# A decoder trunk in split precision: three quarters of the second layer's input turned outside TensorE, and a weight's splits spread out

## The chip, the cores and the metric

The kernel runs on one core of a Trainium2 chip. The metric is device microseconds for one execution of the whole program (two layers); lower is better. Three runs of the kernel before gave 887.66, 887.83 and 887.92 us, median 887.83.

## The reference, cut to what matters

Two layers, each of which maps `x` (256 tokens x 2048 columns) to `LayerNorm(alpha * x + y)`. `y` comes from one wide projection of `x` whose columns go to four groups of heads (retention, latent attention, an mLSTM cell, cross-attention to a fixed memory of 256 tokens), a gate, and one output projection:

```
h = x @ w_in                                   # split into the groups' inputs
cq = rmsnorm(h[a_cq]) ; q = cq @ w_uq          # latent attention: 384 "compressed query" columns, w_uq is 384 x 768
memo = softmax(c_q @ k_mem.T / sqrt(128)) @ v_mem,   k_mem, v_mem = split(mem @ w_mem_kv)
y = (concat(ret, mla, mls, memo) * silu(z)) @ w_out
x = layernorm(2 ** 0.5 * x + y, ln_g, ln_b)    # input of the next layer
```

All values are float32. The second layer needs the first one's normalised output transposed (columns on the partitions), because a matmul contracts over the partitions.

## The kernel before, in words

**Split products.** TensorE multiplies in a rounded 32-bit format. To keep precision each operand is split in a high part (ScalarE rounds it by a copy) and a low part (VectorE subtracts the high part from the operand), and each product is three matmuls: high x high, low x high, high x low.

**Chunks and tiles.** The weights of a layer are streamed as a row of chunks: `memv` (tiles 0 to 15), `memk` (16 to 31), the feature-major halves `lx0 lx1 cq0 cq1` (32 to 63), `akv` (64 to 79, 256 columns wide), `aq` (80 to 95, 328 wide), `lv` (96 to 111), `lo` (112 to 127) and so on, 304 tiles a layer. A tile is 128 rows of a chunk, in most chunks 512 columns wide. SP loads two tiles at a time (a pair, number m holds tiles 2m and 2m + 1) into a buffer of four pairs, in order, together with all other transfers. ScalarE writes a tile's high part (L1095), VectorE its low part (L1446), into rings of five tiles; TensorE uses them in order (L1357, L1358 for the high part, L1361 for the low one; L1372 and L1378 in the feature-major chunks). A slot of the ring is written again when TensorE is through with it. So ScalarE and VectorE run ahead of TensorE by less than five tiles, and every engine works strictly in the order of its own program.

**An order written out by hand.** All other work is a set of steps that are put behind numbered tiles: `PE_AT`, `ACT_AT` and `DVE_AT` give for each engine the tile behind whose own work a step stands (`FIRST_` and `LATER_` hold for one layer alone). Steps at the same tile run in the order in which `_put` entered them. Steps that matter here, with their tiles:
- `wuq` k (k = 0, 1, 2): the copy L937 on ScalarE (behind tiles 45, 46, 47) and the subtraction L1566 on VectorE (behind 46, 47, 48) that split a third of the compressed queries' weight, 128 x 768 values. The product that needs all three (`mla_qr`) stands behind tile 132.
- `ml_fold` (L1179 on TensorE behind 72, copied out by ScalarE, L1004, behind 77).
- the memory heads h = 0 to 3: `mem_scores` on TensorE behind 71, 75, 81, 87; `mem_max` on VectorE (L1587, L1589) behind 76, 80, 86, 92; `mem_exp` on ScalarE (L954) behind 78, 82, 88, 94; `mem_norm` on VectorE (L1594, L1597) behind 80, 84, 90, 96; a turn of each head on VectorE (L1578) behind 81, 85, 93, 97. ScalarE's `mem_pT` copies behind 102, 103, 110 and 111 wait for a transfer. VectorE's `turn c` stands behind 109.

**The second layer's input.** The first layer's output `X` (two halves of 128 tokens, four column blocks of 512) is normalised by ScalarE in eight steps (`normalise`, L868) behind tiles 8 to 15 of the second layer, while TensorE works on the memory chunks, which don't need it. Columns 0 to 1023 are turned by TensorE: steps `xT` 0 and 1 behind tile 18, `xT` 2 and 3 behind tile 22, each four transposes of 128 x 128 (L1131) into one bank of `work`. Columns 1024 to 2047 go another way: VectorE turns each 32 x 32 square in place (`square_x` 2 and 3, L1517, two instructions each), SP writes the result to DRAM (behind pairs 10 and 11) and reads it back with the squares in their places (behind pairs 14 and 15, four reads of 32 partitions each, after both writes have landed). ScalarE then makes `xx`'s high part (`x_hi` j behind tiles 23, 24, 27, 28, 29, 30, 32, 33, L890: gain and bias of the norm in the same instruction) and VectorE the low part (`x_lo` j behind tiles 24 to 37, L1500, L1509), j running over blocks of 256 columns. The chunk `lx0` is the first that needs them.

Of the kernel before, what the change touches and what calls it, by code (L numbers as in the profile page):

```python
# [29 lines left out]
F32 = mybir.dt.float32  # L30
# [6 lines left out]
P = 128  # L37
DEPTH = 2
D_MODEL = 2048
SEQ = 256  # L40
# [93 lines left out]

for _j in range(4):
    _put(LATER_PE, 18 + _j // 2 * 4, "xT", _j)
# [18 lines left out]
for _j in range(8):  # L155
    _put(LATER_ACT, 8 + _j, "normalise", (4, 5, 6, 7, 0, 1, 2, 3)[_j])
    _put(LATER_ACT, (23, 24, 27, 28, 29, 30, 32, 33)[_j], "x_hi", _j)
    _put(FIRST_ACT, 15 + 2 * _j, "x_hi", _j)
    if _j:
        _put(FIRST_ACT, 2 * _j - 1, "m_hi", _j + 1)  # L160
# [26 lines left out]
DVE_AT = {}  # L187
_put(LATER_DVE, 11, "square_x", 2)
_put(LATER_DVE, 13, "square_x", 3)
for _j in range(8):  # L190
# [126 lines left out]
def build_trunk(nc, a, out):  # L317
    ctx = ExitStack()
    with ctx:
# [139 lines left out]

        x_squares, x_turned = ([B[i][:, 0:1024] for i in pair] for pair in ((4, 5), (2, 0)))  # L460

        def x_block(j, n):

            return x_turned[j // 2 - 2].rearrange("p (a i j r) -> p j i a r", a=4, i=NT, j=4)[:, j % 2 * 2 + n]

# [80 lines left out]
        scaled, copied = signal("scaled", 0), signal("copied", 0)  # L546
        x_squared, x_turn_out = signal("x_squared", 0), signal("x_turn_out", 0, step=16)
        stored = signal("stored", 0, step=16)
# [134 lines left out]
        def _(sp):  # L683
            for l in range(DEPTH):
                for m in range(PAIRS):
# [61 lines left out]
                    if m == 57:  # L747
# [3 lines left out]
                          .then_inc(mrow_in.sem, 16)  # L751
                    if l and m in (10, 11):
                        sp.wait_ge(x_squared.sem, m - 9)
                        sp.dma_start(a["x_turn"][m - 10], x_squares[m - 10]).then_inc(x_turn_out.sem, 16)
                    if l and m in (14, 15):
                        sp.wait_ge(x_turn_out.sem, 2 * 16)
                        for b in range(4):
                            sp.dma_start(x_turned[m - 14][b * 32:(b + 1) * 32, :].rearrange("c (a n) -> c a n", a=4),
                                         a["x_turn"][m - 14, :, b * 256:(b + 1) * 256].rearrange("(a c) n -> c a n", a=4))\
                              .then_inc(xT_in[m - 12].sem, 16)  # L760
# [79 lines left out]
        def _(act):  # L840
# [20 lines left out]
            for l in range(DEPTH):  # L861

                def normalise(b):
                    cb, i = divmod(b, 2)
                    blk = X[:, i, cb * 512:(cb + 1) * 512]
                    if b == 4:
# [10 lines left out]
                def x_hi_(j):  # L877
                    if l == 0:
                        act.wait_ge(xT_in[j // 2].sem, 16)
                        act.activation(xh[:, 2 * j:2 * j + 2, :], xT0[:, j, :].rearrange("p (k t) -> p k t", k=2),  # L880
                                       ACT.Copy).then_inc(x_hi.sem, 1)
                        return
                    if j < 4:
                        wait_job(act, l, ("xT", j))
                    else:
                        act.wait_ge(xT_in[j // 2].sem, 16 + 4 * 16)
                    act.wait_ge(cols_in.sem, cols_in.at(l, 0))
                    for k in (2 * j, 2 * j + 1):
                        o, f = xh[:, k, :], (bank(l, ("xT", j))[:, (k % 2) * 256:(k % 2 + 1) * 256] if j < 4 else x_block(j, k % 2))
                        m = act.activation(o if j < 4 else o.rearrange("p (i a r) -> p i a r", i=NT, a=4), f, ACT.Identity,  # L890
                                           scale=cols[:, C_LNG + k:C_LNG + k + 1], bias=cols[:, C_LNB + k:C_LNB + k + 1])
                    m.then_inc(x_hi.sem, 1)
# [223 lines left out]
        def _(pe):  # L1116
# [5 lines left out]
            for l in range(DEPTH):  # L1122
# [295 lines left out]
        def _(dve):  # L1418
# [49 lines left out]
            for l in range(DEPTH):  # L1468
# [23 lines left out]
                def x_lo_(j):  # L1492
                    dve.wait_ge(x_hi.sem, x_hi.at(l, j))
                    src, part = xT0[:, j, :].rearrange("p (k t) -> p k t", k=2), xh[:, 2 * j:2 * j + 2, :].bitcast(F32)
                    if l:
                        dve.wait_ge(cols_in.sem, cols_in.at(l, 0))
                        for k in (2 * j, 2 * j + 1):
                            o, f = tmp[:, (k % 2) * 256:(k % 2 + 1) * 256], \
                                (bank(l, ("xT", j))[:, (k % 2) * 256:(k % 2 + 1) * 256] if j < 4 else x_block(j, k % 2))
                            m = dve.tensor_scalar(o if j < 4 else o.rearrange("p (i a r) -> p i a r", i=NT, a=4), f,  # L1500
                                                  cols[:, C_LNG + k:C_LNG + k + 1], cols[:, C_LNB + k:C_LNB + k + 1],
                                                  ALU.mult, ALU.add)
                        if j < 4:
                            m.then_inc(free_bank(l, "xT", j), 1)
                            wait_read(dve, l, ("xT", j))
                        else:
                            link(m)
                        src = tmp[:, :].rearrange("p (k t) -> p k t", k=2)
                    dve.tensor_tensor(xl[:, 2 * j:2 * j + 2, :], src, part, ALU.subtract).then_inc(x_lo.sem, 1)  # L1509
                    if l:  # L1510
                        dve.wait_ge(x_lo.sem, x_lo.at(l, j))

                def square_x(cb):
                    dve.wait_ge(normed.sem, 2 * cb - 2)
                    to = x_squares[cb - 2].rearrange("p (b i j r) -> p i j b r", b=4, i=NT, j=4)
                    for i in range(NT):
# [3 lines left out]
                def gain(b):  # L1520
                    cb, i = divmod(b, 2)
                    blk = X[:, i, cb * 512:(cb + 1) * 512]
                    if b == 0:
                        dve.wait_ge(gb0_in.sem, 16)
                        wait_job(dve, l, ("xT", 3))
                    link(dve.tensor_tensor(blk, blk, gb0[:, 0, cb * 512:(cb + 1) * 512], ALU.mult))
# [585 lines left out]
```

## Time and profile before

| | |
|---|---|
| median of three runs | 887.83 us |
| the profiled execution: its time, its span | 888.09 us, 886.3 us |
| TensorE busy | 880.4 us, 99% of the span |
| VectorE busy | 665.6 us, 75% |
| ScalarE busy | 488.4 us, 55% |
| transfers | 200.33 MB, mean 226 GB/s |

The span runs from the first to the last instruction; the time of the execution holds 1.8 us outside it. Records of successive instructions on one engine overlap by some 0.1 us, on TensorE by more, as its matmuls are pipelined and their ends modelled: what an instruction takes from its engine is read from the distance of two starts. `[2.14 <-PE acc L1361]` behind a row says that the engine stood idle for 2.14 us before it and what ended this.

### The profile page before, as it was taken

How to read it: one execution, taken by the hardware profiler on the slowest of the kernel's cores; microseconds unless marked ns; L12 is line 12 of the kernel's file. 1: busy time of each engine (PE TensorE's matmuls, PEld its weight loads, DVE VectorE, ACT ScalarE, POOL GpSimd, SP SyncE). 2: the span in 40 equal slices, each digit the busy share in tenths (PEclk: the TensorE clock that was granted, in tenths of full speed). 3: DMA queues.
4: the chain of work that ended last, by engine and by line, in shares of the span. 5: the costliest groups of instructions: out<-in, count | busy, mean ns of one | idle time of the engine just before them, and what ended most of it. 6: DMA issues, size and time to landing. Idle time of an engine off the chain costs nothing.

```text
span 886.3 us, 13162 instructions
## 1 busy us (share of the span) xinstructions
PE 880.4 (99%) x4508; PEld 756.2 (85%) x4508; DVE 665.6 (75%) x1326; ACT 488.4 (55%) x914; POOL 18.0 (2%) x18
## 2 busy tenths in 40 slices
PE   9999999999999999999999999999999999999997
PEld 8888998888888888888888889888888888888896
DVE  6869697878695677766679787968777878786765
ACT  6655776545455346544477556755355453565641
POOL 0000000000000000000000000000000001000001
PEclk9999999999999999999999999999999999999999
DMA  9796487547769677566577866884485865867832
GB/s 358 294 324 205 135 263 257 185 141 222 225 222 312 216 245 256 199 198 194 194 237 232 297 252 176 267 261 167 144 266 163 278 228 161 289 218 258 320 89 95
DMA packets 72402, 200.33 MB, mean 226 GB/s; under 512 B 9608, under 2 KB 24208, under 8 KB 71696
## 3 DMA queue, kind: packets, MB, share of 16 engines
q1 hardware_dynamic: 71760, 198.44, 67.9%
q10 hardware_dynamic: 576, 1.05, 0.4%
q8 instruction: 36, 0.59, 0.3%
q14 instruction: 30, 0.25, 0.1%
HBM read 183.43 MB, written 16.00 MB: 225 GB/s over the span
## 4 chain that ended last, share of the span: by engine, by line
PE 98%; issue 1%; DMA 0%; ACT 0%; POOL 0%; DVE 0%; POOLq 0%; ACTq 0%; DVEq 0%
PE acc L1357 24%; PE acc L1358 24%; PE acc L1361 24%; PE acc L1372 10%; PE acc L1378 5%; PE work L1138 1%; PE work L1137 1%; PE work L1136 1%; PE work L1262 1%; DMA B<-in_mem_t 0%; PE work L1285 0%; PE work L1274 0%; PE work L1194 0%; PE work L1188 0%; PE acc L1398 0%
## 5 line engine op out<-in xcount | busy, mean ns | idle before, releaser
L1095 ACT ACTIVATE hi<-raw 128x512 fp32r<-128x512 f32 (+2 forms) x607 | 356.3, 604 | 300.3 <-PE acc L1361 242.5
L1446 DVE TENSOR_TENSOR lo<-raw,hi 128x512 fp32r<-128x512 f32 (+2 forms) x607 | 387.2, 655 | 176.7 <-ACT hi L1095 167.8
L1357 PE MATMUL acc<-hi,xx 128*128 128x512 f32 (+2 forms) x768 | 285.5, 374 | 0.0
L1358 PE MATMUL acc<-hi,xx 128*128 128x512 f32 (+2 forms) x768 | 283.6, 372 | 0.0
L1361 PE MATMUL acc<-lo,xx 128*128 128x512 f32 (+2 forms) x768 | 223.0, 372 | 0.0
L1357 PEld LDWEIGHTS acc<-hi,xx 128*128 128x128 f32 x768 | 144.6, 188 | 23.6
L1358 PEld LDWEIGHTS acc<-hi,xx 128*128 128x128 f32 x768 | 144.6, 188 | 23.6
L1361 PEld LDWEIGHTS acc<-lo,xx 128*128 128x128 f32 x768 | 140.4, 188 | 24.6
L1372 PE MATMUL acc<-xx,hi 128*128 128x512 f32 x384 | 96.0, 392 | 0.0
L1372 PEld LDWEIGHTS acc<-xx,hi 128*128 128x128 f32 x384 | 69.3, 189 | 12.6
L1378 PEld LDWEIGHTS acc<-xx,lo 128*128 128x128 f32 x384 | 52.4, 190 | 3.7
L1378 PE MATMUL acc<-xx,lo 128*128 128x256 f32 x384 | 53.5, 282 | 0.0
L1357 PE MATMUL acc<-hi,mm 128*128 128x512 f32 x126 | 49.2, 391 | 0.0
L1358 PE MATMUL acc<-hi,mm 128*128 128x512 f32 x126 | 49.0, 389 | 0.0
L1361 PE MATMUL acc<-lo,mm 128*128 128x512 f32 x126 | 38.8, 389 | 0.0
L1361 PEld LDWEIGHTS acc<-lo,mm 128*128 128x128 f32 x126 | 23.6, 188 | 5.0
L1357 PEld LDWEIGHTS acc<-hi,mm 128*128 128x128 f32 x126 | 23.7, 188 | 4.8
L1358 PEld LDWEIGHTS acc<-hi,mm 128*128 128x128 f32 x126 | 23.7, 188 | 4.8
L816 POOL TENSOR_TENSOR rstd<-stats,half 128x4 f32<-128x4 f32 (+1 forms) x6 | 9.6, 1594 | 349.0 <-DVE stats L1899 220.5
L997 ACT ACTIVATE B<-work 128x512 f32<-128x512 f32 x12 | 7.2, 596 | 14.7 <-PE work L1138 14.7
L1622 DVE SCALAR_TENSOR_TENSOR B<-B,cols 128x256 f32<-128x256 f32 x24 | 11.6, 482 | 0.6
L1358 PE MATMUL acc<-hi,B1r 128*128 128x512 f32 (+1 forms) x32 | 12.0, 377 | 0.0
(355 smaller groups left out, 960.1 us busy)
## 6 DMA issues: line engine op xcount, KB each, us to landing
raw<-in_w SPq DMA_DIRECT2D x263, 512.0 KB, 4.3
B<-turn SPq DMA_DIRECT2D x80, 128.0 KB, 4.6
raw<-in_w SPq DMA_DIRECT2D x26, 256.0 KB, 2.7
turn<-B SPq DMA_DIRECT2D x12, 512.0 KB, 5.8
raw<-in_w SPq DMA_DIRECT2D x16, 328.0 KB, 3.3
turn<-Y SPq DMA_DIRECT2D x8, 512.0 KB, 5.6
Y<-in_wuq SPq DMA_DIRECT2D x2, 1152.0 KB, 8.3
Y<-in_x_t SPq DMA_DIRECT2D x4, 512.0 KB, 8.7
```

Of the source, the lines that this page charges most:

```text
L816: return pool.tensor_tensor(dst, src, half[:, 0:n], ALU.pow)
L1095: act.activation(place(l, t, hi), raw[:, s, (t % 2) * w:(t % 2 + 1) * w], ACT.Copy)\
L1136: pe.matmul(o, ah, bh, start=start, stop=False)
L1137: pe.matmul(o, al, bh, start=False, stop=False)
L1138: return pe.matmul(o, ah, bl, start=False, stop=stop)
L1357: pe.matmul(o, ah[:, q], hi[:, s, 0:w], start=k == 0, stop=False, skip_group_check=name == "memv")
L1358: pe.matmul(o, al[:, q], hi[:, s, 0:w], start=False, stop=False, skip_group_check=name == "memv")
L1361: m = pe.matmul(acc[:, p, i, 0:w], ah[:, i * P:(i + 1) * P], lo[:, s, 0:w], start=False, stop=k == KT - 1, skip_group_check=name == "memv")
L1372: pe.matmul(acc[:, p, j, :], hi[:, (l * SLOTS + t + u) % RING, q], x, start=k + u == 0 and kk == 0, stop=False, skip_group_check=True)
L1378: m = pe.matmul(acc[:, p, j, 0:SEQ], lo[:, s, q], both_parts[:, 2 * k + kk, 0, :], start=False, stop=2 * k + kk == KT - 1, skip_group_chec ...
L1446: dve.tensor_tensor(place(l, t, lo), raw[:, s, (t % 2) * w:(t % 2 + 1) * w], place(l, t, hi).bitcast(F32), ALU.subtract).then_inc(lo_done. ...
L1622: m = dve.scalar_tensor_tensor(xcT[:, j, :], LX[:, j, tap:tap + SEQ], wcol, xcT[:, j, :], ALU.mult, ALU.add)
```

## The change

It does two things. The column block 512 to 1023 of the second layer's input takes the way of squares and DRAM as well, so that three blocks go that way and TensorE turns only columns 0 to 511 (`xT` 0 and 1). The normalisation begins with the blocks that go this way; the squares stand behind tiles 10, 12 and 14, the writes behind pairs 10, 11 and 12, the reads behind pairs 13, 14 and 15, each of which waits for its own block's write alone. `xT` waits for all eight normalisations.

And in both layers the three splits of the compressed queries' weight move: the copies to tiles 77, 108 and 118, the subtractions to tiles 79, 109 and 120. They are entered after the other steps at the same tile (`ml_fold` at 77 on ScalarE, `turn c` at 109 and `ml_gap` 3 at 120 on VectorE).

```diff
-for _j in range(4):
+for _j in range(2):
     _put(LATER_PE, 18 + _j // 2 * 4, "xT", _j)
...
-    _put(LATER_ACT, 8 + _j, "normalise", (4, 5, 6, 7, 0, 1, 2, 3)[_j])
+    _put(LATER_ACT, 8 + _j, "normalise", (2, 3, 4, 5, 6, 7, 0, 1)[_j])
...
-_put(LATER_DVE, 11, "square_x", 2)
-_put(LATER_DVE, 13, "square_x", 3)
+for _cb in range(1, 4):
+    _put(LATER_DVE, 8 + 2 * _cb, "square_x", _cb)
...
 for _k in range(3):
-    _put(ACT_AT, 45 + _k, "wuq", _k)
-    _put(DVE_AT, 46 + _k, "lo", "wuq", _k)
+    _put(ACT_AT, (77, 108, 118)[_k], "wuq", _k)
+    _put(DVE_AT, (79, 109, 120)[_k], "lo", "wuq", _k)
...
-        x_squares, x_turned = ([B[i][:, 0:1024] for i in pair] for pair in ((4, 5), (2, 0)))
+        x_squares, x_turned = ([B[i][:, 0:1024] for i in pair] for pair in ((4, 5, 6), (7, 2, 0)))
...
-                    if l and m in (10, 11):
+                    if l and m in (10, 11, 12):
                         sp.wait_ge(x_squared.sem, m - 9)
-                        sp.dma_start(a["x_turn"][m - 10], x_squares[m - 10]).then_inc(x_turn_out.sem, 16)
-                    if l and m in (14, 15):
-                        sp.wait_ge(x_turn_out.sem, 2 * 16)
+                        sp.dma_start(a["x_turn"][m - 10], x_squares[m - 10]).then_inc(x_turn_out[m - 10].sem, 16)
+                    if l and m in (13, 14, 15):
+                        sp.wait_ge(x_turn_out[m - 13].sem, 16)
                         for b in range(4):
...
-                    if j < 4:
+                    if j < 2:
                         wait_job(act, l, ("xT", j))
                     else:
                         act.wait_ge(xT_in[j // 2].sem, 16 + 4 * 16)
...
-                    pe.wait_ge(normed.sem, 2 * (j // 2) + 6)
+                    pe.wait_ge(normed.sem, 2 * (j // 2) + 8)
```

## Rows read from the trace of the kernel before

**Rows 1.** Busy time by engine, page part 1, cut to its one line.

```profile
PE 880.4 (99%) x4508; PEld 756.2 (85%) x4508; DVE 665.6 (75%) x1326; ACT 488.4 (55%) x914; POOL 18.0 (2%) x18
```

**Rows 2.** TensorE's waits: us in total, times, longest.

```profile
PE work L1120 <- DVE half L1420: 1.1, 1, 1.1
...
```

**Rows 3.** TensorE's timeline, layer 2, tiles 17 to 19: start us, us, instructions.

```profile
464.33 0.39 PE L1357 MATMUL acc<-hi,mm 128*128 128x512 f32 x1
...
465.69 1.04 PE L1131 MATMUL work<-ident,X 128*128 128x128 f32 x8
...
467.95 0.40 PE L1357 MATMUL acc<-hi,mm 128*128 128x512 f32 x1
```

**Rows 4.** Instructions of line 1131: duration ns least/median/most, first and last start.

```profile
L1131 PE MATMUL work<-ident,X x16: 270/272/273, 465.7 to 472.8; 128*128 128x128 f32 x16
```

**Rows 5.** VectorE's timeline, layer 2, squares behind tile 13.

```profile
453.56 1.30 DVE L1517 STREAM_TRANSPOSE B<-X 128x512 f32<-128x512 f32 x2
...
455.67 0.69 DVE L1446 TENSOR_TENSOR lo<-raw,hi 128x512 fp32r<-128x512 f32 x1 [0.24 <-ACT hi L1095]
```

**Rows 6.** SP's timeline, layer 2: the first turned block is read back.

```profile
465.55 2.80 SPq L758 DMA_DIRECT2D B<-x_turn  x4
```

**Rows 7.** DMA issues: count, KB each, median us from issue to landing.

```profile
B<-x_turn SPq DMA_DIRECT2D x8, 128.0 KB, 4.9
```

**Rows 8.** ScalarE's timeline, layer 2, behind tile 27.

```profile
472.79 1.00 ACT L890 ACTIVATE xx<-work,cols 128x256 fp32r<-128x256 f32 x2
```

**Rows 9.** ScalarE's timeline, layer 1: splits at tiles 46 and 47; tiles 77 to 79.

```profile
66.23 0.83 ACT L937 ACTIVATE Xr<-Y 128x768 fp32r<-128x768 f32 x1
66.97 0.62 ACT L1095 ACTIVATE hi<-raw 128x512 fp32r<-128x512 f32 x1
...
102.81 0.60 ACT L1004 ACTIVATE B<-work 128x512 f32<-128x512 f32 x1 [0.48 <-PE work L1179]
103.58 0.42 ACT L1095 ACTIVATE hi<-raw 128x256 fp32r<-128x256 f32 x1 [0.17 <-PE acc L1361]
...
106.23 1.51 ACT L1095 ACTIVATE hi<-raw 128x256 fp32r<-128x256 f32 x4
```

**Rows 10.** VectorE's timeline, layer 1: tiles 46, 47, 79 to 81, 91.

```profile
67.23 0.95 DVE L1566 TENSOR_TENSOR Yr<-Y,Xr 128x768 fp32r<-128x768 f32 x1
68.09 0.69 DVE L1446 TENSOR_TENSOR lo<-raw,hi 128x512 fp32r<-128x512 f32 x1
...
106.68 0.86 DVE L1446 TENSOR_TENSOR lo<-raw,hi 128x256 fp32r<-128x256 f32 x2 [2.22 <-ACT hi L1095]
107.46 0.16 DVE L1594 RECIPROCAL rinv<-rsum 128x2 f32<-128x2 f32 x1
...
108.98 0.50 DVE L1446 TENSOR_TENSOR lo<-raw,hi 128x328 fp32r<-128x328 f32 x1
...
118.87 0.90 DVE L1446 TENSOR_TENSOR lo<-raw,hi 128x328 fp32r<-128x328 f32 x2
```

**Rows 11.** TensorE's timeline, layer 1: low parts of tiles 81 and 91.

```profile
109.87 0.46 PE L1361 MATMUL acc<-lo,xx 128*128 128x328 f32 x2
...
120.31 0.46 PE L1361 MATMUL acc<-lo,xx 128*128 128x328 f32 x2
```

**Rows 12.** VectorE's timeline, layer 2: low parts of tiles 81, 111, 121.

```profile
544.31 0.50 DVE L1446 TENSOR_TENSOR lo<-raw,hi 128x328 fp32r<-128x328 f32 x1
...
580.59 0.69 DVE L1446 TENSOR_TENSOR lo<-raw,hi 128x512 fp32r<-128x512 f32 x1 [2.01 <-ACT hi L1095]
...
597.26 1.29 DVE L1446 TENSOR_TENSOR lo<-raw,hi 128x512 fp32r<-128x512 f32 x2 [1.11 <-ACT hi L1095]
```

**Rows 13.** TensorE's timeline, layer 2: low part of tile 81.

```profile
545.20 0.46 PE L1361 MATMUL acc<-lo,xx 128*128 128x328 f32 x2
```

**Rows 14.** ScalarE's timeline, layer 2, behind tiles 110 and 118.

```profile
579.40 0.63 ACT L937 ACTIVATE pTh<-B 128x512 fp32r<-128x512 f32 x1 [3.62 <-DMA B<-turn]
...
591.60 0.63 ACT L1095 ACTIVATE hi<-raw 128x512 fp32r<-128x512 f32 x1 [2.14 <-PE acc L1361]
```

More of the change, by code:

```diff
@@ L458, in build_trunk @@
         early = [Br[i][:, :].rearrange("p (a k t) -> p a k t", a=2, k=2) for i in (1, 2, 3, 0)]
-        x_squares, x_turned = ([B[i][:, 0:1024] for i in pair] for pair in ((4, 5), (2, 0)))
+        x_squares, x_turned = ([B[i][:, 0:1024] for i in pair] for pair in ((4, 5, 6), (7, 2, 0)))
         def x_block(j, n):
-            return x_turned[j // 2 - 2].rearrange("p (a i j r) -> p j i a r", a=4, i=NT, j=4)[:, j % 2 * 2 + n]
+            return x_turned[j // 2 - 1].rearrange("p (a i j r) -> p j i a r", a=4, i=NT, j=4)[:, j % 2 * 2 + n]
         def y_part(part, j):
@@ L546, in build_trunk @@
         scaled, copied = signal("scaled", 0), signal("copied", 0)
-        x_squared, x_turn_out = signal("x_squared", 0), signal("x_turn_out", 0, step=16)
+        x_squared, x_turn_out = signal("x_squared", 0), [signal(f"x_turn_out{cb}", 0, step=16) for cb in (1, 2, 3)]
         stored = signal("stored", 0, step=16)
@@ L751, in _ @@
                           .then_inc(mrow_in.sem, 16)
[L752 removed]
+                    if l and m in (10, 11, 12):
                         sp.wait_ge(x_squared.sem, m - 9)
[L754 to L756 removed]
+                        sp.dma_start(a["x_turn"][m - 10], x_squares[m - 10]).then_inc(x_turn_out[m - 10].sem, 16)
+                    if l and m in (13, 14, 15):
+                        sp.wait_ge(x_turn_out[m - 13].sem, 16)
                         for b in range(4):
[L758 to L759 removed]
+                            sp.dma_start(x_turned[m - 13][b * 32:(b + 1) * 32, :].rearrange("c (a n) -> c a n", a=4),
+                                         a["x_turn"][m - 13, :, b * 256:(b + 1) * 256].rearrange("(a c) n -> c a n", a=4))\
                               .then_inc(xT_in[m - 12].sem, 16)
@@ L865, in normalise @@
                     blk = X[:, i, cb * 512:(cb + 1) * 512]
-                    if b == 4:
+                    if b == 2:
                         act.wait_ge(ln_done.sem, ln_done.at(l, -1))
@@ L888, in x_hi_ @@
                     for k in (2 * j, 2 * j + 1):
-                        o, f = xh[:, k, :], (bank(l, ("xT", j))[:, (k % 2) * 256:(k % 2 + 1) * 256] if j < 4 else x_block(j, k % 2))
-                        m = act.activation(o if j < 4 else o.rearrange("p (i a r) -> p i a r", i=NT, a=4), f, ACT.Identity,
+                        o, f = xh[:, k, :], (bank(l, ("xT", j))[:, (k % 2) * 256:(k % 2 + 1) * 256] if j < 2 else x_block(j, k % 2))
+                        m = act.activation(o if j < 2 else o.rearrange("p (i a r) -> p i a r", i=NT, a=4), f, ACT.Identity,
                                            scale=cols[:, C_LNG + k:C_LNG + k + 1], bias=cols[:, C_LNB + k:C_LNB + k + 1])
@@ L1498, in x_lo_ @@
                             o, f = tmp[:, (k % 2) * 256:(k % 2 + 1) * 256], \
-                                (bank(l, ("xT", j))[:, (k % 2) * 256:(k % 2 + 1) * 256] if j < 4 else x_block(j, k % 2))
-                            m = dve.tensor_scalar(o if j < 4 else o.rearrange("p (i a r) -> p i a r", i=NT, a=4), f,
+                                (bank(l, ("xT", j))[:, (k % 2) * 256:(k % 2 + 1) * 256] if j < 2 else x_block(j, k % 2))
+                            m = dve.tensor_scalar(o if j < 2 else o.rearrange("p (i a r) -> p i a r", i=NT, a=4), f,
                                                   cols[:, C_LNG + k:C_LNG + k + 1], cols[:, C_LNB + k:C_LNB + k + 1],
                                                   ALU.mult, ALU.add)
-                        if j < 4:
+                        if j < 2:
                             m.then_inc(free_bank(l, "xT", j), 1)
@@ L1513, in square_x @@
                 def square_x(cb):
-                    dve.wait_ge(normed.sem, 2 * cb - 2)
-                    to = x_squares[cb - 2].rearrange("p (b i j r) -> p i j b r", b=4, i=NT, j=4)
+                    dve.wait_ge(normed.sem, 2 * cb)
+                    to = x_squares[cb - 1].rearrange("p (b i j r) -> p i j b r", b=4, i=NT, j=4)
                     for i in range(NT):
@@ L1524, in gain @@
                         dve.wait_ge(gb0_in.sem, 16)
-                        wait_job(dve, l, ("xT", 3))
+                        wait_job(dve, l, ("xT", 1))
                     link(dve.tensor_tensor(blk, blk, gb0[:, 0, cb * 512:(cb + 1) * 512], ALU.mult))
@@ L2105 @@
     args["turn"] = nc.dram_tensor("turn", (len(TURNS), P, 4 * SEQ), F32, kind="Internal").ap()
-    args["x_turn"] = nc.dram_tensor("x_turn", (2, P, 4 * SEQ), F32, kind="Internal").ap()
+    args["x_turn"] = nc.dram_tensor("x_turn", (3, P, 4 * SEQ), F32, kind="Internal").ap()
     args["mrow"] = nc.dram_tensor("mrow", (HEADS, SEQ), F32, kind="Internal").ap()
```

## The prediction, made before the change was built

> **What bounds the kernel now.** I read the busy times first, then TensorE's waits, then its timeline. TensorE is busy 880.4 of 886.3 us [rows 1], its longest recorded wait is 1.1 us, at the very start [rows 2], and between warm-up and tail the starts of its matmuls keep an unbroken beat: in the memory stage of the second layer one tile (one 128-row slice of a weight chunk, numbered 0 to 303 in each layer) takes 465.69 - 464.33 = 1.36 us [rows 3]. So the time is the sum of what TensorE issues. Work taken off TensorE is gained in full; work moved between the other engines costs nothing until a high part (ScalarE) or a low part (VectorE) of a tile comes after TensorE wants it. The reader has to look for two things: how much TensorE work goes, and where the lead of the other engines is thinnest. The second decides.
>
> **The turns that leave TensorE.** Steps xT 2 and 3 go: eight 128x128 transposes in one group behind tile 22 of layer 2. Their twin, xT 0 and 1 behind tile 18, starts at 465.69, and the same place of the next tile comes at 467.95: 2.26 us against 1.36 without transposes, so a group costs 0.90 us [rows 3]. Nothing stands beside it, TensorE being the bound: **-0.90 us**. The record of each transpose is 272 ns long [rows 4], but records overlap, so the starts count. The Trainium skill (TensorE: Matmul & The Clock Gate, Part 4: PE-mode transpose) says that such a transpose takes about 275 ns inside a kernel, most of it access latency. The trace agrees on the length and not on the cost in a row of eight; by that page's figure the gain would be an estimated 8 x 0.275 = 2.2 us and my sum would end at 887.5 us.
>
> **What takes their place.** Two more 32x32 square transposes on VectorE, one more 512 KB write and four more 128 KB reads on SP's queue. The squares stood behind tiles 11 and 13, now behind 10, 12 and 14. A pair takes about 1.2 us, and with it VectorE still waits 0.24 us for ScalarE's next tile [rows 5]; each pair again has two tile times, so no lag piles up: 0 (without that cover 1.2 us, one pair). ScalarE does the same eight normalisations in the same places, only columns 512 to 2047 first; xT 0 and 1 now want all eight, the last issued with tile 15, three tiles ahead of their turn: 0. In SP's queue the first block's reads now stand behind pair 13, one pair (2.72 us) ahead of the 465.55 us at which the second block's begin [rows 6], so at about 462.8. Issuing four took 2.80 us and a read lands in 4.9 us [rows 6, 7]: 470.5 at the latest. ScalarE wants the block at 472.79 [rows 8]: 2.3 us to spare, and behind that ScalarE's own lead. SP's new waits (a write must have landed before it is read back) each come three pairs after the write, as before; behind them stand weight loads, issued four pairs ahead. I take 0; below zero it cannot go, as nothing waits there today, and above I keep it as a rival. The high and low parts of the second column block now read SBUF instead of PSUM, on engines with lead: 0.
>
> **The splits that move.** Each layer splits the compressed queries' weight in three: a copy on ScalarE, then a subtraction on VectorE. Where they stood (tiles 45 to 48) TensorE never waited, so taking them away gains 0. Where they go:
>
> Second and third (copies behind 108 and 118, subtractions behind 109 and 120). In layer 2, ScalarE waits 3.62 us for a transfer before the next head's weights and 2.14 us for TensorE behind tile 118 [rows 14]; VectorE waits 2.01 us ahead of tile 111 and 1.11 us ahead of tile 121 [rows 12]. A copy takes 0.74 us of ScalarE (66.97 - 66.23, [rows 9]) and a subtraction 0.86 us of VectorE (68.09 - 67.23, [rows 10]). Both fit: 0. Layer 1 has the same order.
>
> First (copy behind tile 77, subtraction behind tile 79). Here the chunk is narrow, so TensorE takes its tiles faster, and the two other engines are busy with the memory heads. Step by step in layer 1:
> - ScalarE cannot start earlier: tile 77's step ml_fold, which stands ahead of the new copy, waits for TensorE and starts at 102.81, 0.60 long [rows 9]. With the overlap that successive records show (0.83 long, next after 0.74: 0.09), the copy starts at 103.32 and tile 78's high part at 104.06 instead of 103.58: **0.48 us late**. Behind it stand the exponential of head 0 and tile 79's high part (106.23), without a gap, so this is 0.48 late too.
> - VectorE waits for that high part, so the low part of tile 79 starts at 107.16 instead of 106.68 [rows 10]. The subtraction goes between it and tile 80's low part: another 0.86. The reciprocal of head 0 comes at 107.46 + 1.34 = 108.80. Tile 80's low part comes just about in time; if not, that wait is part of the one that follows.
> - From there to tile 81 VectorE has no gap (reciprocal, scaling, maximum of head 1). Its low part ran from 108.98 for 0.50 us and ended 0.39 us before TensorE took it at 109.87 [rows 10, 11]. Now it ends at 110.82. TensorE waits 1.34 - 0.39 = **0.95 us**, with the scores of head 2 and every later tile behind it. Nothing gives this back.
>
> Layer 2 has the same steps: tile 81's low part starts at 544.31, TensorE takes it at 545.20 [rows 12, 13], again 0.39 us of lead, so 0.95 us again. The trace has no wait of TensorE on VectorE to price the waking of it, so I bound each wait. Low: ScalarE's copy hides fully and only 0.86 counts, 0.47 us a layer. High: both full lengths, 0.83 + 0.95 = 1.78, less 0.39, 1.39 us a layer. I take 0.95, from the distances of starts.
>
> **The sum.** -0.90 + 2 x 0.95 = +1.00 us. On the profiled execution (888.09 us, 1.8 us of it outside the span of 886.3) that is 889.1; it stands 0.26 us above the median of the runs, so on 887.83 it is **888.8 us**, 0.11% slower. By the bounds: 887.9 (+0.04) to 889.7 (+1.88). A measurement of this kernel can tell about 0.2% (1.8 us) from no change, so I forecast no measurable change: a gain eaten by a thin place elsewhere.
>
> **Rivals.**
> - No wait at tile 81: the whole 0.90 us stays, **886.9 us**. It asks that VectorE do the subtraction before tile 79's high part comes. Speaking for it: VectorE is idle just there, 2.22 us [rows 10]. Against: its program puts the subtraction behind tile 79's low part, which needs that high part.
> - The other side, slower by more than 0.2%: the lag grows between tiles 82 and 91. Place: ScalarE's exponentials and VectorE's maxima of heads 1 to 3 wait for one another with no idle time on VectorE. Tile 91's low part starts at 118.87, ends some 0.49 us later and is taken at 120.31, 0.95 us of lead [rows 10, 11]. As VectorE is 1.34 late and TensorE 0.95, 0.56 is left. It decides from the point at which these hand-offs add more than 0.56 us. If they repeat the first lag, each layer loses 1.34 - 0.56 = 0.78 more: **890.4 us**. For it: four hand-offs and not one pause. Against: every link of that chain is shifted alike, none is lengthened.
> - The first block comes late. ScalarE then stands at its split of that block with all later tiles behind it. TensorE feels it once the lead is used up: the ring holds five tiles of 1.36 us, I take three, 4 us, thus from a landing at about 477, some 14 us after the issue; each further us costs one. With 2 us so lost, 890.8 us. Against: eight reads of this kind run there today in 4.9 us [rows 7]. The Trainium skill (VectorE: DVE Perf Modes, The three transpose paths) warns that a plain DMA copy that transposes by strides is 19 times slower than the crossbar's 1.3 us; by an estimate from that page a block would take 25 us, the landing be near 488 and the time near 900. The 4.9 us of these reads, which move whole rows of squares, speak against it.
>
> **Chances.** Forecast 0.64 (its own range 887.9 to 889.5); no wait 0.14; lag grows 0.14; late block 0.05, of which 0.01 for the page's 25 us; 0.03 for what I don't see, 0.02 of it faster. The forecast and the first rival lie within 0.2%: 0.78. Slower by over 0.2%: 0.14 + 0.05 + 0.01 = 0.20. Faster by over 0.2% would need 1.8 us off TensorE, twice what the change removes: 0.02. Range 886.9 to 890.4, from the first rival to the second; outside lie the late block, the surprises and half of the second rival's tail, some 0.15.
>
> **What would show it.** TensorE's transposes of x: 8 instead of 16. In both layers a wait of TensorE at tile 81 for VectorE's low part, near 110 and 545 us, about a microsecond less what modelled matmul ends hide; ScalarE's copy of 768 columns right behind ml_fold, tile 78's high part half a microsecond later, the subtraction between the low parts of 79 and 80. Nothing at tiles 85 to 91, 111 and 121, and no wait of ScalarE for a turned block near 473 us. Wrong if TensorE shows no wait near 110 us (then about 886.9), or one more behind tile 82.

## The result, and the profile after

The kernel after took 889.67 us (median of 13 runs, 888.98 to 891.33), the kernel before on the same chip 887.78 (13 runs). The ratio is 1.0021, with a 95% interval of 1.0013 to 1.0029. The forecast was 888.8 with a range of 886.9 to 890.4: the time is inside, 0.9 us above the value. The interval does not reach 1, so these runs do tell the change from none; "no measurable change", with its mark at 0.2%, was a little too modest. The runs also lie further apart than before: 2.35 us, where 11 of the 13 of before lie within 0.6. Here and below, a few executions that stand far out are left aside: three of milliseconds (two of before, one of transfers_only) and one of load_33_reads, 970.76 us at a granted clock of 0.851.

The profiled run took 889.39 us (span 887.6), 1.30 more than that of before. First TensorE's transposes of x (duration in ns least/median/most, first and last start), in answer to [rows 4]:

```profile
L1131 PE MATMUL work<-ident,X x8: 272/272/273, 466.5 to 467.2; 128*128 128x128 f32 x8
```

Eight transposes are gone. In the trace of every kernel without them TensorE has gained 0.89 to 0.90 us on before by the place behind the group. TensorE's waits, with us in total, times and longest, answer [rows 2]; a line is there that before did not have:

```profile
PE acc L1361 <- DVE lo L1446: 1.5, 2, 0.8
```

TensorE's timeline shows where, in layer 1 and in layer 2 [rows 11, 13]:

```profile
109.45 0.32 PE L1358 MATMUL acc<-hi,xx 128*128 128x328 f32 x1
110.53 0.57 PE L1361 MATMUL acc<-lo,xx 128*128 128x328 f32 x2 [0.77 <-DVE lo L1446]
110.94 0.28 PE L1136 MATMUL work<-B0r,B2r 128*128 128x256 f32 x1
...
545.33 0.31 PE L1358 MATMUL acc<-hi,xx 128*128 128x328 f32 x1
546.41 0.56 PE L1361 MATMUL acc<-lo,xx 128*128 128x328 f32 x2 [0.78 <-DVE lo L1446]
546.82 0.28 PE L1136 MATMUL work<-B0r,B2r 128*128 128x256 f32 x1
```

The low part of tile 81 starts 1.08 us behind the matmul ahead of it; the usual distance is 0.15 (109.30 to 109.45). That is 0.93 us, and the pair that waited takes 0.41 instead of 0.30 to the next start: **1.04 us in each layer**. The recorded idle time (0.77) is less, because the modelled end of the matmul ahead covers a part of it, so the starts count.

What ScalarE and then VectorE did ahead of it in layer 1 [rows 9, 10]:

```profile
102.52 0.60 ACT L1004 ACTIVATE B<-work 128x512 f32<-128x512 f32 x1 [0.48 <-PE work L1179]
103.02 0.84 ACT L937 ACTIVATE Xr<-Y 128x768 fp32r<-128x768 f32 x1
103.75 0.41 ACT L1095 ACTIVATE hi<-raw 128x256 fp32r<-128x256 f32 x1
...
106.39 1.51 ACT L1095 ACTIVATE hi<-raw 128x256 fp32r<-128x256 f32 x4
```

```profile
106.83 0.42 DVE L1446 TENSOR_TENSOR lo<-raw,hi 128x256 fp32r<-128x256 f32 x1 [2.22 <-PE acc L1361]
107.17 0.95 DVE L1566 TENSOR_TENSOR Yr<-Y,Xr 128x768 fp32r<-128x768 f32 x1
108.04 0.49 DVE L1446 TENSOR_TENSOR lo<-raw,hi 128x328 fp32r<-128x328 f32 x1
...
109.98 0.50 DVE L1446 TENSOR_TENSOR lo<-raw,hi 128x328 fp32r<-128x328 f32 x1
```

This is the chain of the forecast, link by link: the copy right behind ml_fold, the subtraction between the low parts of tiles 79 and 80, and the low part of tile 81 ending at 110.48, just before TensorE takes it.

One thing was not forecast. In layer 2 TensorE starts 0.27 us late at 493.69 us and loses another 0.11 behind that, 0.38 us in all. ScalarE waits longer for weights; its waits, the first line of before, the second of after:

```profile
ACT hi L1095 <- DMA raw<-in_w: 12.6, 20, 1.9
```

```profile
ACT hi L1095 <- DMA raw<-in_w: 30.3, 30, 3.5
```

The DMA engines show why. For 455 to 485 us, in 40 slices (tenths of their time), before and then after, with the weight loads and the reads of the turned blocks (count, KB each, median us from issue to landing):

```profile
DMA  8989969997896327948996699999998259405950
...
raw<-in_w SPq DMA_DIRECT2D x10, 512.0 KB, 4.8
```

```profile
DMA  0889999799999999999999999999999998920498
...
raw<-in_w SPq DMA_DIRECT2D x10, 512.0 KB, 6.3
...
B<-x_turn SPq DMA_DIRECT2D x12, 128.0 KB, 6.4
```

Before, the strip has slack between its nines; after, it is full from 458 to 480 us, and what is moved in it lands later: the reads in 6.4 us instead of 4.9 [rows 7], a weight load in 6.3 instead of 4.8 (medians). SP did not issue those loads later: at 465.95 and 472.74, against 465.18 and 471.96 before, when TensorE runs 0.78 us later too.

From there the lateness goes through two engines. ScalarE waits twice for weights among its steps for the second layer's input, for 0.85 us (below) and, ahead of 481.93, for 0.95 us:

```profile
478.85 0.63 ACT L1095 ACTIVATE hi<-raw 128x512 fp32r<-128x512 f32 x1 [0.85 <-DMA raw<-in_w]
```

VectorE, which before has no pause from 475 to 490 us, waits with it and does not make this up. Its last low part of that input (L1509, behind tile 37), before and then after, and the matmuls of after that need it:

```profile
491.50 0.69 DVE L1509 TENSOR_TENSOR xx<-tmp,xx 128x512 fp32r<-128x512 f32 x1
```

```profile
492.95 0.69 DVE L1509 TENSOR_TENSOR xx<-tmp,xx 128x512 fp32r<-128x512 f32 x1
```

```profile
493.69 1.66 PE L1372 MATMUL acc<-xx,hi 128*128 128x512 f32 x6
```

Before, it ended at 492.19, 1.35 us ahead of its matmul at 493.54; after, it ends at 493.64 and the matmul follows at once. That is a second thin place, which the forecast did not price.

The blocks themselves came in time (ScalarE takes the first at 473.57 without a wait [rows 8]), but barely. The forecast took the median of 4.9 us for "at the latest". The reads of before, and then those of the first block after (issue to landing, least/median/most):

```profile
DMA to landing us min/median/max: 3.2/4.9/7.2
```

```profile
DMA to landing us min/median/max: 5.0/5.3/8.1
```

The last of the four, issued at 464.57, landed at 472.7: 0.9 us were to spare, not 2.3.

The account of the profiled run: TensorE is 0.29 us ahead of before by 50 us, a difference at the start that lies between -0.45 and +0.10 in the profiled runs. Then -0.29 - 0.90 + 2 x 1.04 + 0.38 = +1.27, against +1.30 measured.

### The profile page after: what moved, and what is told of

Its sections match the earlier page's. It is cut to its first block, busy times and chain, and to the rows that moved or that the text cites. A ratio compares the mean times of both kernels' runs of the same rounds, so it can differ in the third digit from the quotient of the medians.

```text
span 887.6 us, 13151 instructions
## 1 busy us (share of the span) xinstructions
PE 880.2 (99%) x4500; PEld 755.3 (85%) x4500; DVE 666.1 (75%) x1328; ACT 487.1 (55%) x914; POOL 18.0 (2%) x18
## 2 busy tenths in 40 slices
DMA packets 73122, 201.37 MB, mean 227 GB/s; under 512 B 9688, under 2 KB 24800, under 8 KB 72416
## 3 DMA queue, kind: packets, MB, share of 16 engines
q10 hardware_dynamic: 576, 1.05, 0.4%
## 4 chain that ended last, share of the span: by engine, by line
PE 97%; DVE 1%; issue 1%; ACT 0%; POOL 0%; POOLq 0%; ACTq 0%; DVEq 0%
PE acc L1361 24%; PE acc L1357 24%; PE acc L1358 24%; PE acc L1372 10%; PE acc L1378 5%; PE work L1138 1%; PE work L1137 1%; PE work L1136 1%; PE work L1262 1%; PE work L1120 0%; PE work L1285 0%; PE work L1274 0%; PE work L1194 0%; PE work L1188 0%; DVE lo L1446 0%
## 5 line engine op out<-in xcount | busy, mean ns | idle before, releaser
L1361 PEld LDWEIGHTS acc<-lo,xx 128*128 128x128 f32 x768 | 140.2, 188 | 26.7 <-DVE lo L1446 2.1
```

Of the source, the lines that this page charges most:

```text
L1361: m = pe.matmul(acc[:, p, i, 0:w], ah[:, i * P:(i + 1) * P], lo[:, s, 0:w], start=False, stop=k == KT - 1, skip_group_check=name == "memv")
```

## The experiments

Two questions were open: whether the waits at tile 81 are the splits' alone, and where the 0.7 us above the sum (and the spread) come from. Theory A: the third block's transfers make weights late, by an amount that differs from run to run. Theory B: they cost nothing, as the forecast had it. Each kernel was timed in turn with the kernel before on the same chip, but the kernels ran on five chips: the first four below on one, alloc_only to spread_load on a second, the two with the load at pair 38 on a third, load_33_reads on a fourth, direct_third on a fifth.

**The turns alone** (label turns_only): the kernel after with the splits back in their old places.

```
-    _put(ACT_AT, (77, 108, 118)[_k], "wuq", _k)
-    _put(DVE_AT, (79, 109, 120)[_k], "lo", "wuq", _k)
+    _put(ACT_AT, 45 + _k, "wuq", _k)
+    _put(DVE_AT, 46 + _k, "lo", "wuq", _k)
```

> The changed kernel with the three splits back at tiles 45 to 48; the turns stay changed. Theory A (two waits of 1.04 us at tile 81 come from the moved splits; the turns save 0.90 us, but their 1 MB of further transfers makes the second layer's weights late, by 0.3 us of TensorE in the profiled run and by up to 2 us in others): no wait at tile 81, 16 to 8 transposes, time 887.2 to 888.5, that is -0.6 to +0.7 us against before, with runs spread over 1 us or more, since VectorE has its three subtractions again just where the weights come late. Theory B (the transfers cost nothing, the spread of the changed kernel's runs is that of the chip): 886.9, 0.9 us under before, spread as before.

Measured: 889.54 us, 11 runs from 887.31 to 892.02; before 887.95. No wait at tile 81. The fastest run is near the full gain, the median 2.5 us above it and 1.0 above the range of theory A, which had the lateness too small. The profiled run is one of the longest (891.52), and TensorE's waits in it are of another kind:

```profile
PE acc L1372 <- ACT hi L1095: 1.3, 2, 1.1
...
PE acc L1357 <- ACT hi L1095: 1.0, 2, 0.8
PE acc L1372 <- DVE xx L1509: 0.6, 1, 0.6
```

By starts, it loses 0.29, 1.01, 1.27, 0.39 and 0.97 us at 484, 492, 505, 528 and 585 us, most of it behind transfers that held ScalarE up: weights (2.3 us at 482), the wuq load (3.2 us at 503), a later exchange (7.1 us at 585). With what follows each wait it is 4.4 us: TensorE is 1.01 us ahead of before behind the place of the turns and 3.43 behind it at the end. The profiled runs differ by 891.52 - 888.09 = 3.43. B falls.

**The splits alone** (splits_only): the kernel before with the new places of the splits, the same two lines the other way round.

> The kernel before with only the splits moved. Both theories: two waits of TensorE at tile 81 (near 111 and 547 us), each 0.93 us before the low part and 0.11 behind it, 2 x 1.04 = +2.1 us, 889.9. They differ in the spread: theory A (the spread of the changed kernel comes from its further transfers) expects runs within 0.5 us of each other; theory B (it comes from the splits' new places or from the chip) a spread of 1.5 to 2 us as in the changed kernel.

Measured: 890.03, runs from 889.76 to 890.26; 887.95 + 2 x 1.04 = 890.03. The waits are those of the kernel after, and the runs lie so close together that the spread is none of theirs:

```profile
PE acc L1361 <- DVE lo L1446: 1.6, 2, 0.8
```

**The first subtraction one tile earlier** (subtract_78): the kernel after, in which VectorE has 2.22 us of idle time ahead of tile 79's low part [rows 10].

```
-    _put(DVE_AT, (79, 109, 120)[_k], "lo", "wuq", _k)
+    _put(DVE_AT, (78, 109, 120)[_k], "lo", "wuq", _k)
```

> The changed kernel with the first subtraction behind tile 78 instead of 79, into VectorE's idle time of 2.2 us. Forecast's chain: only ScalarE's lag of 0.48 us reaches tile 81, 0.48 - 0.39 = 0.1 us of wait (0.2 with what follows it) in each layer; against the changed kernel -1.7 us, about 888.0. Rival (the copy on ScalarE makes most of the lag): the waits at tile 81 stay above 0.6 us each and the time above 889.

Measured: 889.15, 887.34 to 890.24. At tile 81 the waits shrink from 1.04 to 0.22 us, as 0.48 of lag against 0.39 of lead says:

```profile
109.40 0.31 PE L1358 MATMUL acc<-hi,xx 128*128 128x328 f32 x1
109.66 0.57 PE L1361 MATMUL acc<-lo,xx 128*128 128x328 f32 x2
110.07 0.28 PE L1136 MATMUL work<-B0r,B2r 128*128 128x256 f32 x1
```

But in the profiled run 2.2 us went in layer 2 between 483 and 507 us. The median stands 1.2 us above that of before, where after stands 1.9 above: 0.7 us gained, not the 1.7 expected.

**The weight loads of the multi-head latent part later** (late_load): the second layer's wukv and wuq loads (1.7 MB) behind pair 28 instead of 22.

```
-                    if m == 22:
+                    if m == (22, 28)[l]:
```

> The changed kernel with the second layer's two loads of the latent attention's weights (1.66 MB, now wanted at tile 77 only) issued behind pair 28 instead of 22. Theory A (the transfers crowd, and a part of the median and the spread is weights that come late near 500 to 512 us): ScalarE's wait for weights near tile 46 (3.45 us) shrinks below 1.5 us, runs within 0.7 us, median 889.0 to 889.3, the two waits at tile 81 unchanged. Theory B (transfers cost nothing): 889.7 and the spread as in the changed kernel.

Measured: 890.24, 889.04 to 892.37, a miss. TensorE loses no more than 0.14 us between 480 and 546 us, tile 81 aside, but 0.7 us at 573 to 585, where ScalarE waits 2.06 us for weights at 557 and for an exchange at 584:

```profile
583.94 0.63 ACT L937 ACTIVATE pTh<-B 128x512 fp32r<-128x512 f32 x1 [6.41 <-DMA B<-turn]
```

The lateness moved and did not go.

**The DRAM buffer alone** (alloc_only): the kernel before with a third, unused block, in case the addresses did it.

```
-args["x_turn"] = nc.dram_tensor("x_turn", (2, P
+args["x_turn"] = nc.dram_tensor("x_turn", (3, P
```

> The kernel before, with one edit: the DRAM buffer of the exchange has three blocks instead of two; the third is never touched. If the spread of the two kernels with the turned third block comes from the addresses that the other buffers then get, this one spreads over more than 2 us as they did, with a median near 888.5 to 889.5. If it comes from the transfers themselves, this one is the kernel before: 887.8 to 888.0, fast runs within 0.6 us of each other.

Measured: 888.20, ten of 11 runs from 887.79 to 888.37 and one of 889.61, before 888.08: the ratio is 1.0000 (0.9991 to 1.0008). Not the addresses.

**The transfers alone** (transfers_only): the kernel before plus the third block's write and reads, whose result is not used.

```
+                    if l and m == 12:
+                        sp.dma_start(a["x_turn"][2], x_squares[1]).then_inc(third.sem, 16)
+                    if l and m == 13:
+                        sp.wait_ge(third.sem, 16)
+                        for b in range(4):
+                            sp.dma_start(B[7][b * 32:(b + 1) * 32, 0:1024]...
+                    if l and m == 25:
+                        sp.wait_ge(third.sem, 5 * 16)
```

> The kernel before, with the transfers of a third block beside its own: the write of the second block's squares into a third DRAM block, four reads into the eighth half-tile buffer one tile later, and a wait for them where the other turned block is waited for. Their result is not used; TensorE still turns sixteen squares. Theory A, that the transfers make later weights late: TensorE's work is that of before, so the time is 887.8 plus the lateness, 0.3 to 3 us, median 888.3 to 890.5, runs 1.5 us or more apart. Theory C, that the moved steps (the low parts of the new block prepared later) make the waits: 887.8 to 888.0 and within 0.6 us.

Measured: 889.82, runs from 887.87 to 891.09, before 888.08: the ratio is 1.002 with an interval of 1.0011 to 1.0029. TensorE, VectorE and ScalarE have exactly the work of before, so 1.7 us and the spread come from what was put into SP's queue: 1 MB of transfers, 0.5% of the program's 200 MB, and one thing that the kernel after has not. The third block's write is waited for one pair after it was issued, not three, and SP stands still for it:

```profile
SPq L761 <- DMA x_turn<-B: 3.9, 1, 3.9
```

The next two weight loads are issued 2.6 and 1.8 us later than before by it (467.43 and 469.81 against 465.18 and 468.39, in a run whose TensorE is 0.40 us ahead). The 1.7 us are therefore not the price of the bytes alone. The profiled run (888.44) is one of the shortest: TensorE loses 0.7 us between 496 and 530 us, 0.42 of it in one wait at 527 us.

**Both waits out of the way** (copy_76): copy behind 76, subtraction behind 78, else the kernel after.

```
-    _put(ACT_AT, (77, 108, 118)[_k], "wuq", _k)
-    _put(DVE_AT, (79, 109, 120)[_k], "lo", "wuq", _k)
+    _put(ACT_AT, (76, 108, 118)[_k], "wuq", _k)
+    _put(DVE_AT, (78, 109, 120)[_k], "lo", "wuq", _k)
```

> The kernel after, with the first split's copy behind tile 76 instead of 77 and its subtraction behind 78 instead of 79. By the forecast's chain the lag of 1.34 us now meets a lead of some 1.8 us, so the waits at tile 81 of both layers go as a whole, 2 x 1.04 = 2.1 us against after, and 0.90 us of turns stay saved: 887.2 to 887.6 if the transfers cost nothing or 0.3 us, up to 889.5 in the runs where they do. Runs 1.5 us or more apart, median near 888. If the waits at 81 were not what costs the time, it stays at 889.3 to 889.9.

Measured: 888.65, 887.19 to 889.17, ratio 1.0001 (0.9992 to 1.0009). Nothing is left at tile 81; the fastest run is the sum, 888.08 - 0.90 = 887.18, and the median 1.5 above it. In the profiled run (887.40) 0.40 us go at 492 us, behind the same last low part as in the kernel after.

**Loads set further apart** (spread_load): copy_76 with the load at pair 28, the gate-weight load (2 MB) at pair 70 instead of 32, and the last low part of the block one tile earlier.

```
-                    if m == 22:
+                    if m == (22, 28)[l]:
-                    if l == 1 and m == 32:
+                    if l == 1 and m == 70:
-    _put(LATER_DVE, (24, 26, 28, 30, 32, 33, 35, 37)[_j], "x_lo", _j)
+    _put(LATER_DVE, (24, 26, 28, 30, 32, 33, 35, 36)[_j], "x_lo", _j)
```

> The kernel after, with copy and subtraction behind tiles 76 and 78, the second layer's wukv and wuq loads at tile 28 instead of 22, the gate-weight load behind them at tile 70 instead of 32, and the last low part of the new block prepared one tile earlier. If the lateness of the weights comes from large loads that stand close together behind the turned blocks, these now stand apart: no wait for weights near 485 to 505 us and none near 557 to 589, so 887.83 - 0.90 + 0 to 0.4 = 886.9 to 887.3, runs within 0.8 us. If the crowding only moves again, 887.5 to 889.5 and spread.

Measured: 888.49, 887.36 to 892.02: the fastest runs are near the sum, and the runs lie 4.7 us apart. The profiled run (887.62) has one wait left from the stretch, at 492 us, 0.79 us by starts; with the last low part of the input one tile earlier it is now a weight's low part that comes late:

```profile
PE acc L1378 <- DVE lo L1446: 0.6, 1, 0.6
```

**The load at pair 38** (load_38), and with it **the second and third block read one pair later** (load_38_reads: `m in (13, 15, 16)` for `(13, 14, 15)`):

```
-                    if m == (22, 28)[l]:
+                    if m == (22, 38)[l]:
```

> The run with the spread-out loads, with one number changed: the second layer's wukv and wuq loads stand at weight pair 38 instead of 28, some 28 us later, where the copies leave the DMA engines less busy. Its profile lost 0.82 us at 509.8 us, just behind that load; if the load's nearness to the turned blocks is what makes weights late, that loss goes: 886.9 to 887.6 and runs within 1 us. If the third block's own transfers near 464 to 476 us are enough, the wait near 492 us stays, and the time is 887.4 to 889 with runs 1.5 us or more apart.

> As the run with the load at pair 38, with the reads of the second and third turned blocks one pair (some 2.8 us) later, so that a pair without reads lies behind the first block's. If the reads' crowding between 464 and 476 us (DMA share 1.07 in the kernel after, 0.83 before) makes the weights late, the wait near 492 us gets smaller or goes: 886.9 to 887.3, runs within 0.8 us. If the reads only come later and the steps that read the blocks now wait for them, 887.5 to 889.

Measured (five runs each): 891.16 (889.88 to 892.67) and 892.50 (889.39 to 894.78), both misses. The reason to move the load had been misread: the loss of 0.82 us that the expectation names was a group of matmuls cut in two by the edge of a stretch of the timeline; read in one piece, the beat at 510 us is whole. And the place is bad for a plain reason, seen in ScalarE's timeline of the second kernel: at 531 us the load is issued too near to the first split's copy, which waits for it. TensorE then loses 1.81 and 0.52 us at 543 and 546 us; the first kernel loses 3.8 us there, and 1.05 at 492 us as well.

```profile
538.90 0.85 ACT L938 ACTIVATE mm<-Y 128x768 fp32r<-128x768 f32 x1 [3.59 <-DMA Y<-in_wuq]
```

**The load at pair 33, reads later** (load_33_reads):

> As the run with the load at pair 38 and the later reads, with the load at pair 33. The profile of that run lost nothing over 0.4 us between 464 and 530 us, and 1.82 and 0.53 us at 541 to 546 us, where the first split's copy waited 3.6 us for the wuq load issued at 531.3 us. At pair 33 it is issued near 520 us, so that wait goes: 889.39 - 1.82 - 0.53 = 887.04 for a run like the profiled one, median 886.9 to 887.6, and runs within 1 us if the reads' place was what is left of the spread. If the lateness of weights moves with the load once more, 888 to 890 and runs 2 us or more apart.

Measured: 889.04, 886.96 to 890.68. The wait for wuq is gone; now ScalarE waits 3.6 us for the turned blocks, and TensorE waits 0.5 us at 484 and 1.0 us at 493 (0.8 and 1.2 by starts):

```profile
PE acc L1379 <- DVE lo L1447: 1.0, 1, 1.0
PE acc L1373 <- ACT hi L1096: 0.5, 1, 0.5
```

None of the kernels in which transfers were only moved in time lost its spread.

**Fewer bytes, and none of the third block's through DRAM** (direct_third): copy_76, with the last of the three blocks moved straight between its two SBUF buffers, without the DRAM block.

```
-                    if l and m in (10, 11, 12):
+                    if l and m in (10, 11):
...
+                    if l and m in (12, 15, 16, 17):
+                        sp.wait_ge(x_squared.sem, 3)
+                        a_ = (12, 15, 16, 17).index(m)
+                        for b in range(4):
+                            sp.dma_start(x_turned[2][b * 32:(b + 1) * 32, a_ * 256:(a_ + 1) * 256],
+                                         x_squares[2][a_ * 32:(a_ + 1) * 32, b * 256:(b + 1) * 256]).then_inc(xT_in[3].sem, 16)
-                    if l and m in (13, 14, 15):
+                    if l and m in (13, 14):
```

> The run with copy and subtraction behind tiles 76 and 78, with one of the three blocks (the last) exchanged straight from its squares to the half-tile buffer that takes it, without the DRAM block between: sixteen transfers of 32 KB, four each at pairs 12, 15, 16 and 17, in place of one write of 512 KB and four reads of 128 KB. It moves 0.5 MB less than that run, so the DMA share of 464 to 476 us lies between 0.83 (before) and 1.07. If the lateness of weights follows the bytes moved beside them, the spread falls to about half and the median to 887.3 to 888.0. If the number of transfers and packets decides, which does not fall, it stays at 888.3 to 889.

Measured: **886.90**, 9 of 11 runs from 886.77 to 887.22; before 887.80 (887.66 to 888.38). Ratio 0.9992 (0.9983 to 1.0001): the interval just reaches 1, but those 9 runs lie below the fastest of before. The other two took 887.82 and 888.26, so the spread is not quite gone; before has 0.72 us in 15 runs. The whole gain of the turns is there: 887.80 - 0.90 = 886.90. The same stretch of the DMA engines as above:

```profile
DMA  6979999999979899999999997967796397678169
...
raw<-in_w SPq DMA_DIRECT2D x10, 512.0 KB, 5.2
...
B<-B SPq DMA_DIRECT2D x16, 32.0 KB, 3.4
```

The strip has slack again from 474 us on, weights land in 5.2 us, and TensorE loses nothing over 0.1 us behind the place of the turns. The moved steps of the third block are all in this kernel, so they by themselves cost nothing. It moves 0.5 MB less (200.85 MB against 201.37), moves the block's parts later, and takes the block off DRAM, all at once. Later reads alone (load_33_reads) kept the spread, so the bytes or the way through DRAM are the likelier reason, but no run parts them. And no kernel with the third block through DRAM ran on this chip. The medians of before lie within 0.4 us of each other in all comparisons, which speaks against the chip as the reason, but does not rule it out.

## Why the prediction was right, and which term was not

All kernels against the sum of TensorE's parts (the median of before in the same comparison, -0.90 for the turns, the waits at tile 81 as read from starts):

| kernel | sum | fastest | median | median over sum |
|---|---|---|---|---|
| after | 887.78 - 0.90 + 2.08 = 888.96 | 888.98 | 889.67 | 0.7 |
| turns_only | 887.95 - 0.90 = 887.05 | 887.31 | 889.54 | 2.5 |
| splits_only | 887.95 + 2.08 = 890.03 | 889.76 | 890.03 | 0.0 |
| subtract_78 | 887.95 - 0.90 + 0.44 = 887.49 | 887.34 | 889.15 | 1.7 |
| late_load | 887.95 - 0.90 + 2.08 = 889.13 | 889.04 | 890.24 | 1.1 |
| alloc_only | 888.08 | 887.79 | 888.20 | 0.1 |
| transfers_only | 888.08 | 887.87 | 889.82 | 1.7 |
| copy_76 | 888.08 - 0.90 = 887.18 | 887.19 | 888.65 | 1.5 |
| spread_load | 888.08 - 0.90 = 887.18 | 887.36 | 888.49 | 1.3 |
| load_38 | 888.12 - 0.90 = 887.22 | 889.88 | 891.16 | 3.9 |
| load_38_reads | 888.12 - 0.90 = 887.22 | 889.39 | 892.50 | 5.3 |
| load_33_reads | 888.00 - 0.90 = 887.10 | 886.96 | 889.04 | 1.9 |
| direct_third | 887.80 - 0.90 = 886.90 | 886.77 | 886.90 | 0.0 |

Every kernel's fastest run is its sum within 0.3 us, but for the two with the load at pair 38, which have waits of their own near 543 us. The medians are 0.7 us and more above it in the kernels with a third block through DRAM, and only there.

That the time fell into the range is in part luck. The forecast rise of 1.00 us was 1.89 by the medians. The waits gave 0.18 of the difference; the other 0.7 come from a term that stood at 0. The high bound of the forecast's own sum, 889.7, just reaches the median, and the 890.4 above it was the price of a lag that did not grow.

- *The turns that leave TensorE, -0.90*: right, shown by the starts in every trace and by direct_third, where nothing else that costs time is left of the change. The Trainium skill (TensorE: Matmul & The Clock Gate, Part 4: PE-mode transpose) gives about 275 ns for one of bf16; by that the estimate was 2.2 us for eight. The records here, of f32, are 272 ns long, but the eight cost 0.90.
- *The first split, 2 x 0.95*: right in place, chain and nearly in size. Copy, tile 78 and subtraction stand where the forecast put them; it measured 1.04 a layer, since a group of matmuls that has waited takes 0.11 us longer, which no row of before shows for this group. (The forecast says that before has no wait of TensorE on VectorE; [rows 2] has one, at the very start, of another group.) The rival with no wait is refuted by the waits themselves; that the price was these waits and nothing else is shown by splits_only (+2.08) and, from the other side, by the traces of subtract_78 (0.22 left at tile 81) and copy_76 (nothing left).
- *Second and third fit, and no growth behind tile 82*: right. By starts TensorE loses nothing at tiles 82 to 91, 111 and 121, in either layer.
- *What takes their place, "I take 0"*: the term that was mis-sized. It measured 0.38 us in the profiled run and 0.7 in the median of after; turns_only and copy_76 have 2.5 and 1.5. The argument looked at the moved block (2.3 us to spare by the median read, 0.9 in fact) and not at what shares the DMA engines with it: ten weight loads of 512 KB in the same 30 us, which land 1.5 us later in the median. It also gave VectorE lead without a number; the last low part of the input had 1.35 us. The windows of before had the warning: the DMA share (next to last in the rows below) was 0.86 and 0.83 around the moved block, and 0.95 at 500 to 512 us, which leaves little room for 1 MB more. After, 464 to 476 us stand at 1.07 and 500 to 512 us at 1.02 (the share adds up packets by their start, so a stretch can exceed 1). The third rival had the cause (transfers late, ScalarE held up, TensorE behind it) but the wrong victim: weights and later loads, at 483 to 590 us, not the block at 473. The rows are of before, then of after:

```profile
452.00:464.00 12.00, 12.00 (x55) 9.93 (x54) 8.09 (x14) 8.06 (x13) 0.00 (x0) 1.00 0.86 278
464.00:476.00 12.00, 12.00 (x63) 10.08 (x62) 10.38 (x18) 7.85 (x15) 0.00 (x0) 1.00 0.83 221
```

```profile
464.00:476.00 12.00, 12.00 (x58) 10.00 (x57) 10.68 (x18) 8.33 (x16) 0.00 (x0) 1.00 1.07 293
```

- The page's rule in that rival, a transposing copy 19 times slower (the Trainium skill, VectorE: DVE Perf Modes, The three transpose paths), did not come in: the twelve reads, which move whole rows of squares, landed in 6.4 us in the median, 9.7 at most. The page's 1.3 us is for 128 x 128 values of bf16, a sixteenth of a block of 512 KB, so the estimate of 25 us was one for that sixteenth and not for a block.

What stays open: why runs of one kernel differ by up to 5 us once the DMA engines are full, and whether direct_third owes its steadiness to fewer bytes, to their place in time, or to the way past DRAM. That the DMA engines set the lateness is read from traces of single runs (after, turns_only); how much of each kernel's median it makes is inferred from the sums, not traced run by run.

## What to carry to other kernels

Work moved off the bound engine onto DMA has two prices: when its own transfer lands, and how much later everything else in those queues lands; read the DMA share by windows, and the slowest landing and not the median, before calling it free. A step put between two other engines costs by the thinnest lead behind it, and that lead can be read to a tenth of a microsecond from the starts of before. When medians spread, compare the fastest runs with the sum of the known terms: what is left over is the part that varies.

## What was not expected of the hardware

- With one more MB among 200 MB, and the wait for its write, runs of the same program lay 3.2 us apart (transfers_only); 30 of 33 runs of before in the same comparison lie within 1.03 us.
- Sixteen SBUF-to-SBUF transfers of 32 KB landed in 3.4 us (median) and cost SP 0.60 us each to issue (2.41 us for four, three times out of four); the four 128 KB reads of a block from DRAM took SP from 1.85 us to 3.01 us.
- ScalarE's waits for weights by themselves don't tell the time: direct_third has 26.7 us of them, after 30.3, before 12.6. The sum of these waits does not tell how much of them reaches TensorE: nothing in direct_third behind the place of the turns, 0.38 us in after.
- A waiting group of two 328-column matmuls took 0.41 us to the next start instead of 0.30, in both layers.
